# Attention of a hybrid diffusion step: probabilities divided by their sums on VectorE before they are turned, and scores issued ahead of the turning

## What is computed

```python
def attend_block(qs):
    qn, qr = qs
    s = jnp.einsum("bqhd,bkhd->bhqk", qn, k_nope) + jnp.einsum("bqhr,bkr->bhqk", qr, k_rope)
    p = jax.nn.softmax(s.astype(jnp.float32) * ATTN_SCALE, axis=-1).astype(v.dtype)
    return jnp.einsum("bhqk,bkhd->bqhd", p, v)
```

## Time and profile before

| What | Value |
|---|---|
| Median of 3 runs | 1317.88 us (1314.31 to 1322.88) |
| The profiled execution's own time | 1319.29 us |
| Its span | 1317.4 us |
| TensorE busy | 1229.0 us (93% of the span) |
| VectorE busy | 641.1 us (49%) |
| ScalarE busy | 396.1 us (30%) |
| GpSimd busy | 176.5 us (13%) |

### The profile page before, as it was taken

The page is one execution under the profiler, slowest core; times in us unless marked ns, Lnnn a source line. Parts: engine busy times, 40 slices in busy tenths (PEclk is TensorE's granted clock), DMA queues, the critical chain, the costliest instruction groups (busy, mean ns, idle before and its releaser), DMA issues.

```text
span 1317.4 us, 18862 instructions
## 1 busy us (share of the span) xinstructions
PE 1229.0 (93%) x6976; PEld 821.9 (62%) x6977; DVE 641.1 (49%) x1347; ACT 396.1 (30%) x730; POOL 176.5 (13%) x172
## 2 busy tenths in 40 slices
PE   4899999899999989999999999999989999999992
PEld 1454555455545688888878555556664568888881
DVE  1365978253326633333332578784542654333333
ACT  2100213344433213332223002135554321332233
POOL 4000102130200011222220000021210001222220
PEclk9999999899999889999999999999999989999996
DMA  9883330855481639989995000102007154999976
GB/s 368 265 329 133 67 121 23 301 181 182 148 296 66 221 99 330 288 228 336 302 260 167 0 4 1 57 23 106 1 1 272 64 187 151 327 336 313 326 191 191
DMA packets 139386, 239.31 MB, mean 182 GB/s; under 512 B 23394, under 2 KB 106304, under 8 KB 133184
## 3 DMA queue, kind: packets, MB, share of 16 engines
q1 hardware_dynamic: 120736, 186.70, 41.6%
q0 software_dynamic: 11712, 28.73, 9.7%
q10 hardware_dynamic: 6880, 23.08, 4.4%
HBM read 216.10 MB, written 31.82 MB: 188 GB/s over the span
## 4 chain that ended last, share of the span: by engine, by line
PE 55%; DMA 28%; DVE 7%; issue 5%; ACT 3%; DVEq 1%; ACTq 0%; POOLq 0%; SPq 0%
PE ps L1317 26%; DMA x_rows<-region_proj,row_out 23%; PE ps L1596 9%; PE ps L1487 4%; DMA region_h<-in_w_ada 3%; PE ps L1509 3%; PE ps L1342 3%; PE ps L1520 3%; DVE region_proj L1304 2%; PE ps L1589 1%; DVE region_h L869 1%; DMA x<-x_rows 1%; PE ps L1488 1%; PE ps L1498 1%; ACT region_weights L744 1%
## 5 line engine op out<-in xcount | busy, mean ns | idle before, releaser
L976 DVE SCALAR_TENSOR_TENSOR region_bc<-region_conv,vecs,region_bc 128x655 f32<-128x655 f32 x240 | 202.0, 904 | 0.9
L1317 PE MATMUL ps<-region_h,region_weights 128*128 128x128 f32 (+1 forms) x512 | 139.7, 434 | 1.5 <-ACT region_h L677 1.5
L1317 PEld LDWEIGHTS ps<-region_conv,region_weights 128*128 128x128 f32 x1088 | 124.0, 192 | 10.0 <-issue 7.2
L1317 PEld LDWEIGHTS ps<-region_conv,region_oq 128*128 128x128 f32 x1088 | 124.1, 192 | 8.2 <-issue 8.1
L1317 PE MATMUL ps<-region_conv,region_weights 128*128 128x128 f32 x1088 | 124.4, 275 | 2.4 <-DVE region_conv L1282 2.4
L1317 PE MATMUL ps<-region_conv,region_oq 128*128 128x128 f32 x1088 | 124.3, 275 | 0.0
L1317 PEld LDWEIGHTS ps<-region_h,region_weights 128*128 128x128 f32 x512 | 77.6, 191 | 65.5 <-issue 63.7
L1057 DVE TENSOR_REDUCE att_stat<-ps 128x1 f32<-128x640 f32 (+1 forms) x68 | 55.5, 816 | 116.8 <-PE ps L1488 111.9
L869 DVE TENSOR_TENSOR region_proj<-ps,region_proj 128x128 f32<-128x128 f32 (+1 forms) x89 | 27.8, 312 | 157.0 <-ACT region_proj L842 140.1
L1317 PE MATMUL ps<-region_oq 128*128 128x512 f32 (+2 forms) x304 | 94.2, 471 | 2.7 <-issue 2.1
L842 ACT ACTIVATE region_proj<-ps 128x128 f32<-128x128 f32 x68 | 18.9, 278 | 252.5 <-PE ps L1317 252.5
(11 more groups left out here) (229 smaller groups left out, 1694.8 us busy)
## 6 DMA issues: line engine op xcount, KB each, us to landing
region_h<-in_w_ada SPq DMA_DIRECT2D x26, 1024.0 KB, 5.0
region_oq<-in_w_ada SPq DMA_DIRECT2D x20, 1024.0 KB, 8.9
region_weights<-in_w_gate SPq DMA_DIRECT2D x16, 1024.0 KB, 8.8
region_weights<-in_w_up SPq DMA_DIRECT2D x16, 1024.0 KB, 13.4
region_weights<-in_w_down SPq DMA_DIRECT2D x16, 1024.0 KB, 15.6
region_oq<-in_w_gate SPq DMA_DIRECT2D x16, 1024.0 KB, 9.4
region_oq<-in_w_up SPq DMA_DIRECT2D x16, 1024.0 KB, 14.2
region_oq<-in_w_down SPq DMA_DIRECT2D x16, 1024.0 KB, 16.2
```

Source lines behind the costliest of these rows:

```text
L976: ins = nc.vector.scalar_tensor_tensor(acc[:, ct, :], zpad[:, ct, j:j + CONV_OUT], w, acc[:, ct, :], ALU.mult, ALU.add)
L1317: ins = nc.tensor.matmul(out, lhs(k), rhs(k), start=(k == 0), stop=(k == n - 1))
```

## The change

VectorE no longer inverts the sums of a group for TensorE to spread. For each unit it takes the reciprocal of its sums and multiplies the 128x640 probabilities (128x512 for a context unit) by it in place, two units behind the maximum (`scale`). TensorE turns a unit when it has been multiplied, and now issues the scores of unit i+2 ahead of the turning of unit i. The spreading matmuls, the ScalarE copy for the context units and the waits for them are gone, the copies are 640 columns wide, and the output is a copy instead of a product. ScalarE's order stays: the copy of unit i and then the exponential of i+1.

```diff
 # ScalarE
 def turned(i):
...
-                    if g >= 3 and i % 2 == 0:
-                        act.wait_ge(att_out_empty, GROUPED * l + g - 2)
-                    if g < LAT_GROUPS:
-                        n = LAT_KEYS + (P if i % 2 == 0 and g >= 1 else 0)
-                    else:
-                        n = 4 * P + (P if i % 2 == 0 else 0)
+                    n = LAT_KEYS if g < LAT_GROUPS else 4 * P
...
-                act.wait_ge(ctx_spread, l + 1)
-                act.wait_ge(att_out, GROUPED * l + LAT_GROUPS)
-                nc.scalar.activation(probT[2][:, 0:4 * P], ps[:, 5], ACT.Copy).then_inc(ctx_spread_ready, 1)
 # VectorE
-                def inverse_sums(g):
-                    dve.wait_ge(att_exp, UNITS * l + 2 * g + 2)
-                    cols = slice(2 * g, 2 * g + 2) if g < LAT_GROUPS else slice(2 * LAT_GROUPS, STATS)
-                    nc.vector.reciprocal(s_inv[:, cols], s_sum[:, cols]).then_inc(sums_inverted, 1)
+                def scale(i):
+                    h, t, cols = unit_parts(i)
+                    dve.wait_ge(att_exp, UNITS * l + i + 1)
+                    step(nc.vector.reciprocal(s_inv[:, cols], s_sum[:, cols]))
+                    if t < LAT:
+                        ins = nc.vector.tensor_scalar(prob[:, i % 2], prob[:, i % 2], s_inv[:, cols], None, ALU.mult)
+                    else:
+                        p4 = prob[:, i % 2, 0:4 * P].rearrange("p (h n) -> p h n", h=4)
+                        ins = tt(p4, p4, s_inv[:, cols].unsqueeze(2).broadcast_to([P, 4, P]), ALU.mult)
+                    ins.then_inc(prob_scaled, 1)
...
-                        tt(attT[:, pr, t * P:(t + 1) * P], ps[:, 6, 0:P], spread, ALU.mult).then_inc(att_out_empty, 1)
+                        nc.vector.tensor_copy(attT[:, pr, t * P:(t + 1) * P], ps[:, 6, 0:P]).then_inc(att_out_empty, 1)
...
                 for i in range(UNITS):
-                    if i % 2 == 1 and i >= 3:
-                        inverse_sums((i - 3) // 2)
+                    if i >= 2:
+                        scale(i - 2)
                     maximum(i)
...
-                inverse_sums(LAT_GROUPS)
+                scale(UNITS - 2)
+                scale(UNITS - 1)
 # TensorE
                 def turn_prob(i):
                     g = i // 2
-                    pe.wait_ge(att_exp, UNITS * l + i + 1)
+                    pe.wait_ge(prob_scaled, UNITS * l + i + 1)
...
-                    if i % 2 == 0 and g >= 1:
-                        ins = spread(g - 1, flat[:, 2048 + n * P:2048 + (n + 1) * P], 2 * g - 2)
...
                 for i in range(UNITS):
-                    turn_prob(i)
                     if i + 2 < UNITS:
                         score(i + 2)
+                    turn_prob(i)
...
-                for k in range(4):
-                    ins = spread(LAT_GROUPS, ps[:, 5, k * P:(k + 1) * P], 2 * LAT_GROUPS + 2 * k)
-                ins.then_inc(ctx_spread, 1)
...
-                pe.wait_ge(ctx_spread_ready, l + 1)
```

More of the change, by code:

```diff
@@ L216, in hybrid_step_kernel @@
         base += 2 * LAT_KEYS
[L217 to L220, removed]
+        probT = [None, None, PR[:, 4 * TOK:4 * TOK + LAT_KEYS], None]
+        for n in (0, 1, 3):
+            probT[n] = W1[:, base:base + LAT_KEYS]
+            base += LAT_KEYS
         ln_rstd = W1[:, base:base + CONV_OUT]
@@ L305, in hybrid_step_kernel @@
             sem("prob_turned"), sem("probT_ready"), sem("att_out"), sem("att_out_empty"))
-        sums_inverted, ctx_spread, ctx_spread_ready = sem("sums_inverted"), sem("ctx_spread"), sem("ctx_spread_ready")
+        prob_scaled = sem("prob_scaled")
         conv_step, ln_summed, ln_mean, ln_centred, ln_squared, ln_var, ln_sqrt, ln_rstd_ready, ln_done, conv_silu = (
@@ L1073, in output @@
                         pr, t = divmod(g, LAT)
-                        spread = probT[(2 * g + 2) % 4][:, LAT_KEYS:LAT_KEYS + P] if g < LAT_GROUPS - 1 else probT[0][:, 4 * P:5 * P]
-                        tt(attT[:, pr, t * P:(t + 1) * P], ps[:, 6, 0:P], spread, ALU.mult).then_inc(att_out_empty, 1)
-                    else:
-                        dve.wait_ge(ctx_spread_ready, l + 1)
-                        tt(attT[:, :, DEC_SEQ:TOK], ps[:, 6].rearrange("p (k n) -> p k n", k=4),
-                           probT[2][:, 0:4 * P].rearrange("p (k n) -> p k n", k=4), ALU.mult).then_inc(att_out_empty, 1)
+                        nc.vector.tensor_copy(attT[:, pr, t * P:(t + 1) * P], ps[:, 6, 0:P]).then_inc(att_out_empty, 1)
+                    else:
+                        nc.vector.tensor_copy(attT[:, :, DEC_SEQ:TOK], ps[:, 6].rearrange("p (k n) -> p k n", k=4)).then_inc(att_out_empty, 1)
                 conv(len(conv_list))
```

## The result

| What | Before | After |
|---|---|---|
| Median | 1319.75 us (4 runs) | 1367.08 us (4 runs, 1366.9 to 1368.27) |
| Ratio | | 1.0372, 95% interval 1.0350 to 1.0393 |
| Span of the profiled execution | 1317.4 us | 1365.1 us |

The account below looks back on a forecast made before the run. TensorE's own work was taken to bound attention, 5.51 us a pair, with the loop through ScalarE 0.40 a unit below. Layer 1 +25.3 and layer 0 +8.1 made +33.4 on 1319.3, less 1.4: forecast 1352 us, range 1339 to 1372.

Parts of the forecast that it names:

- The loop, 3.54 us: Attention, per unit: exponential to turning 2.14 with the scores inside, 0.80 to the copy, 0.60 to the next exponential.
- The hidden branch: VectorE's reciprocal and multiply beside the scores: divided row ready 1.82 us after the exponential's start, hidden with 0.32 cover.
- Layer 1, +25.3: Layer 1's attention: summed loss in us from the longer loop, the start, the root and the context units.
- 23.6 - 2.2 + 0.5 = 21.9: Layer 1, turning 1 to 31: 15 slower pairs +23.6, channel-sum matmuls falling into TensorE's gap -2.2, layer-norm root +0.5.
- +1.0 was predicted: Layer 1's two context units: each gains a reciprocal wait and multiply, loses closing spreads and their copy; an estimate.
- Layer 0, +8.1: Layer 0's attention: summed loss in us, with 24 units carrying a piece of modulation of 0.99.
- VectorE +2, an estimate, with 0 and +5 as its ends: Layer 0: VectorE reads the weighed output, waiting behind a piece, before dividing the next even unit, so cover is short.
- the other terms: Layer 0: pairs with pieces -2.9, scores behind the transfer stall +1.2, four pairs without pieces +6.3, root and context units +1.5.
- The late VectorE: Rival, 9%: VectorE's in-order work outlasts the division's cover, say 0.3 us over 48 units; +15 on top, 1367 us.
- The clock as drawn: Rival, 10%: TensorE's clock falls through pauses in each unit; half the units at the lower level, +35, near 1387 us.
- scores cost little in the loop: Rival, 5%: the attention turning starts at 1.82 after the exponential, the loop is 3.22 us a unit; 1336 us.
- the kernel gets faster: Rival, 3%: TensorE stays the attention's bound at 4.95 us a pair without spreads; -9 a layer, 1300 us.

Follow-up runs that it names:

- e6_turn_first_divide_early: The changed kernel with the turning of i again ahead of the scores of i+2, and VectorE dividing unit i-1 instead of i-2 before maximum i: 1341.4 us.
- e2_turn_first: The changed kernel with TensorE again issuing the turning of i ahead of the scores of i+2, the division kept: 1420.7 us.
- e10_after_chunks_output_late: The changed kernel with GpSimd's layer-norm instructions cut to at most 164 columns and VectorE's output copy moved behind the division: 1349.7 us.

## Why the prediction was right, and where its sum was short

**What bounds it.** Right. A loop through ScalarE replaced TensorE as the bound, and the swap alone, with no division, cost 44 us, of the same size as the whole change's 47.

**The loop, 3.54 us.** Right, measured 3.46. Exponential to scores 0.93 (0.96 predicted), scores 1.18 (1.18), turning to copy 0.75 (0.80), copy to exponential 0.60 (0.60). The multiply took 0.55, as the slope between two other widths gave, and its cover was 0.45 (0.32). The hidden branch, 1.82 from exponential to turning, was put a little high. Its 0.09 to wake TensorE had no row, and its 0.99 came from the unit behind the root. Where the branch binds (`e6_turn_first_divide_early`) it takes 1.71, with the reciprocal 0.91 behind the exponential and 0.05 from the multiply's end to the turning.

**Layer 1, +25.3; measured +30.2.** Up to the turning of unit 1 it is +2.5 (+2.4 predicted). From there to the turning of unit 31 it is +24.9 (before 893.44 to 983.64, after 911.24 to 1026.32), where 23.6 - 2.2 + 0.5 = 21.9 were predicted. The shorter loop takes 2.4 off. The steps that failed: the multiply was costed at 0.55 wherever it stands, and GpSimd makes it up to 1.8. The five units around 935 to 955 took 19.65 instead of 17.3, and the three from unit 25 on 12.72 instead of the 10.78 of the run with cut instructions: +4.3 together, and 0.4 more in the latter three from the output and the layer norm's reciprocals standing ahead of the division. The clock around the root was in no term of the sum. Behind the root, three units took 17.3: 10.4 of loop, 3.7 of root as predicted, and 3.3 of lower clock. The kernel before had 13.53 there (turnings at 953.76 and 967.29), of which 8.66 are its own pace (two even units of 3.15 and an odd one of 2.36), 3.18 the root's stall and 1.7 lower clock. So the lower clock costs 1.6 more than before. It costs 0.5 less at the start, where the kernel before turned unit 1 at the lower level and this one didn't. The last two units stand only 3.27 apart, behind the scores of the context units: -0.4. Together 21.9 - 2.4 + 4.3 + 0.4 + 1.6 - 0.5 - 0.4 = 24.9, the measured +24.9.

From unit 31 to the first projection it is +2.9 where +1.0 was predicted. The last turning, weighing and L1549 took 1.12, 1.08 and 1.98, against 0.66, 0.59 and 0.87 before, 2.1 us more, at a granted clock of 0.50 (last row of the windows above). The earlier trace rows had been the argument that the context units keep their clock. In the kernel before they came behind a stage in which TensorE was busy 94%, and what held there did not hold here.

**Layer 0, +8.1; measured +15.1.** The term "VectorE +2, an estimate, with 0 and +5 as its ends" was mis-sized: moving the output was worth 7.6 us and cutting GpSimd's instructions 0.7 (leaving its work out 4.5). With both done the stage is at +6.7, where the other terms had given 6.1. An undisturbed pair with pieces went from 7.51 to 7.08 (turnings at 290.68 and 297.76), a gain of 0.43 for the predicted 0.29; most other pairs with pieces took 7.8 us or more. The prediction had seen that the output waits behind the piece, and that it stands ahead of the division. It had not put numbers on it: from the start of the piece to the end of the output it is 2.3 us (267.18 to 269.50), and then come a step of the modulation (L859, 0.60) and the division.

**The rivals.** The late VectorE, at 9% and 1367 us, is most of what was added to the forecast, and its time is the measured one. That is luck in part: it had been drawn as 0.3 us over 48 units, from VectorE's own order, while in the undisturbed units nothing was late, GpSimd was not in it, and some 3 us of the measured time are the clock's. With its two causes mended and the rest of the change kept, the kernel took 1349.7, beside a forecast of 1352, with the attention stages at +6.7 and +23.9, beside 6.1 (8.1 without the estimate of 2) and 25.3. The clock as drawn, with half of the units at the lower level, did not come: it was granted in full from 905 to 953 with TensorE busy 71 and 72% and pausing in every unit, and it cost 3.7 us more than before in two short stretches of layer 1 (1.6 behind the root, 2.1 at the end). It did come in `e2_turn_first`, where the loop was another. That scores cost little in the loop, and that the kernel gets faster, are both excluded by the swap alone.

**What stays open.** What lowers the clock over tens of us in `e2_turn_first` and not in the changed kernel, and how much of the 1420.7 is its share. What decides whether one or two units behind the root, or the first of the stage, run at the lower clock: it differs between executions of nearly the same stream. No run separates either. The idle transposes were placed too late to tell.

## What to carry to other kernels

When an instruction moves on an in-order engine, write down every loop that crosses engines, before and after: here a swap of two lines took the scores into one loop (+44 us) and freed another (with the old order and the division +103 us, a good part of it at a lower clock), and the order on the third engine decided between 1420.7 and 1341.4. Where VectorE gets work onto the critical path, look at what GpSimd runs at that time, since the wait hides inside VectorE's own duration, and look for a waiting instruction of low urgency ahead of the urgent one. Removed work on the bound engine pays only after that: with ScalarE's order, GpSimd's lengths and the late output mended it gave 1308.1, 0.95% below the kernel before.

## What the runs showed of the hardware that was not expected

A VectorE multiply of 128x640 takes 0.55 us alone and up to 1.81 beside a GpSimd instruction of 128x655: it ends 0.35 us after GpSimd's has ended, as if only its last part ran then. Cutting GpSimd's instructions to 164 columns bounds it at 0.90 us, and made one kernel 13 us faster (1328.8 to 1315.7, of which 7.9 lie in the attention of the profiles) and another 4.5 (1367.1 to 1362.6), though it adds GpSimd time (178.2 to 191.7 us busy in the former).

TensorE kept its full clock over 48 us with a pause of about 1 us in every unit, and lost it behind the square root, where it was idle for 4.34 us between a weighing and the next scores (991.97): for two units there, and for one in the same place of `e10_after_chunks_output_late`. In `e2_turn_first`, with another loop, the granted clock was 0.71 over 935 to 953 us and 1.00 over 1010 to 1030.
